# In-projection of 24 chunk pairs by seven block products in place of eight, and query norms spread over five heads

## The chip, the core and the metric

The kernel runs on one core of a Trainium2 chip. Its time is the device time of one launch in microseconds (us), lower is better. One execution was also taken by the hardware profiler; all rows below are from it. Engines: PE is TensorE (PEld its weight loads), DVE is VectorE, ACT is ScalarE, POOL is GpSimd; SP only issues transfers (DMAs).

## What is computed

One step of a one-layer hybrid encoder on 1024 prompt tokens and 32 sample tokens (1056 together), width 1024. Everything starts with one wide projection of the normalised, modulated input `h`:

```
h = _rms(x, p['norm_gain']) * (1 + scale[:, None, :]) + shift[:, None, :]
(qkv_raw, z_a, beta_raw, alpha_raw, q_raw, ckv_raw, kr_raw, z_b, g_a, g_b) = _split_in(h @ p['w_in'])
o_a, conv_new, s_new = _deltanet(qkv_raw, beta_raw, alpha_raw, conv_buf, s0, p)
o_b, ckv_new, kr_new = _mla(q_raw, ckv_raw, kr_raw, pos, past_ckv, past_kr, p)
u_a = o_a * jax.nn.silu(z_a)
u_b = o_b * jax.nn.silu(z_b)
merged = jax.nn.sigmoid(g_a) * (u_a @ p['w_o_dn']) + jax.nn.sigmoid(g_b) * (u_b @ p['w_o_mla'])
y = x + gate[:, None, :] * (merged @ p['w_out'])
```

`scale`, `shift` and `gate` come from `c @ w_ada`. `qkv_raw` (3072 columns) also goes through a causal convolution of four taps; the rest of the 9296 columns does not. All data are float32.

## The kernel before

The program runs in stages, and at the end of the first ones all five engines wait for each other (`meet`). **Pass 1** (`*_pass01`) computes the projection transposed, channels on partitions and tokens in columns, and stores it to a scratch in HBM. **Latents** builds keys and values of the attention branch. **Attention** runs 9 query blocks of 8 heads; block i has 128(i+1) keys. Then come the delta branch, the output projections and the result.

In pass 1 a float32 number is held as two parts of the type float32r, a rounded `hi` and the rest `lo`. The input is in `HH` and `HL`; 256 columns of `w_in` (a pair of chunks of 128 channels) come by DMA from POOL's queue into one half of `Wraw`, ACT rounds them into `WH`, DVE subtracts and writes `WL`. A product then takes three matmuls, WL·HH, WH·HL and WH·HH (`pe_chunk`). One chunk is 8 blocks of the inner dimension x 3 parts x 3 PSUM banks of 352 tokens = 72 matmuls, each with its own weight load. There are 73 chunks: 24 with convolution, 48 without, and a narrow one of 80 channels (`MISC`: beta, alpha, rotary key) at the end. Two sets of three PSUM banks alternate. For the 48 plain chunks ACT copies PSUM to `stage` with the activation (line 2249), and SP stores it. For the 24 others ACT copies to `Xr`, DVE convolves (lines 2461 and 2464), ACT applies silu. POOL copies the taps and edges.

The 1024 gate columns of `w_ada` are summed by DVE (`gate_products`, in two halves, early in pass 1) and finished on PE with 16 tiny products (line 2361) after the last plain chunk. The weights `w_uk` and `w_uv` of the latents are also loaded during pass 1; ACT and DVE split `w_uk` there, and `w_uv` at the beginning of latents (lines 341 and 346).

In attention, DVE computes the norms of the next block's queries in three parts (`dve_q_norms`) after heads 2, 3 and 4 of a block (1, 2, 3 of the first), between the row maxima that each head's softmax waits for. PE's first scores of a block wait until both halves of its rotated queries are copied (`s_qe`, line 697).

Of the kernel before, what the change touches and what calls it, by code (L numbers as in the profile page):

```python
# [14 lines left out]
F32 = mybir.dt.float32  # L15
# [6 lines left out]
P = 128  # L22
D = 1024
# [85 lines left out]
def build(nc, a, o, scr, ctx):  # L109
# [17 lines left out]
    p1 = ExitStack()  # L127
    Wraw = sb(p1, "Wraw", [P, 4, KD, 256])
    HH = sb(p1, "HH", [P, KD, TOK], F32R)
    HL = sb(p1, "HL", [P, KD, TOK], F32R)  # L130
    WH = sb(p1, "WH", [P, 2, KD, 256], F32R)
    WL = sb(p1, "WL", [P, 2, KD, 256], F32R)
    R = sb(p1, "R", [P, 9, D])
    rows = sb(p1, "rows", [P, 2, P])
    NHF = 4
    hf = sb(p1, "hf", [P, NHF, 512])
    modr = sb(p1, "modr", [2, 2, 512])
    G = sb(p1, "G", [P, KD, 2])
    xst = sb(p1, "xst", [P, 3, 9])
    Rf = R[:, :, :].rearrange("p a b -> p (a b)")  # L140
# [11 lines left out]
    assert edo + 144 + 2 * P <= 9 * D  # L152
# [15 lines left out]
    s_xn = sem("x_normalised")  # L168
# [28 lines left out]
    gacc = Rf[:, 0:2 * D].rearrange("p (s n) -> p s n", s=2)  # L197
# [111 lines left out]
    def sp_latents(sp):  # L309
        sp_lraw(sp, 0, 0)  # L310
        for t in range(2):
# [20 lines left out]
    def u_raw(i):  # L332

        return Wraw[:, 2 + i % 4 // 2, KR * (i % 2):KR * (i % 2) + KR]
# [13 lines left out]
    def sp_w_u(sp, i):  # L348
        w = a["w_uk"] if i < 4 else a["w_uv"]
        if i >= 4:  # L350
            sp.wait_ge(s_ul, i - 3)
# [133 lines left out]
    def act_latents(act):  # L485
        act.activation(colB[:, B_KN:B_KN + 1], colB[:, B_KN:B_KN + 1], ACT.Copy, scale=colB[:, B_QN:B_QN + 1])
        for i in range(4, 8):
            act_u_hi(act, i)
# [3 lines left out]
        act_lat_hi(act, 0, 0)  # L492
        act_lat_squares(act, 1)
# [54 lines left out]
    def dve_latents(dve):  # L548
# [17 lines left out]
        for i in range(4, 7):  # L566
            dve_u_lo(dve, i)
        dve_latent(dve, 0, 0)
        dve_lat_lo(dve, 0, 0)
        dve_u_lo(dve, 7)  # L570
# [288 lines left out]
    def dve_q_norms(dve, i, part):  # L859

        ss, rs, root = qst[:, 0], qst[:, 1], qst[:, 2]
        if part == 0:
            dve.wait_ge(s_r7, max(turn[("q", i, n)] for n in range(3)) + 1)
            dve.tensor_reduce(ss[:, 0], qsq[:, 0:H * HD].rearrange("p (h n) -> p h n", h=H), AX.X, ALU.add)
            dve.tensor_reduce(ss[:, 1], qsq[:, H * HD:H * QH].rearrange("p (h n) -> p h n", h=H), AX.X, ALU.add)
            dve.drain()
            dve.tensor_scalar(ss[:, 0], ss[:, 0], 1.0 / HD, EPS, ALU.mult, ALU.add)
            dve.tensor_scalar(ss[:, 1], ss[:, 1], 1.0 / ROPE, EPS, ALU.mult, ALU.add)
            dve.drain()
        elif part == 1:  # L870
            if i:
                dve.wait_ge(s_qrr, i)
            rsqrt(dve, rs.rearrange("p a b -> p (a b)"), root.rearrange("p a b -> p (a b)"), ss.rearrange("p a b -> p (a b)"))
# [79 lines left out]
    def dve_attention(dve):  # L953
# [3 lines left out]
        for x in range(NX + 3):  # L957
# [1073 lines left out]
    def sp_pass01(sp):  # L2031
# [8 lines left out]
        for c in range(2):  # L2040
            sp.wait_ge(s_adam, 7 + c)
            w_ada(2 + c, 2 * D + 256 * c)
# [3 lines left out]
        def stores(first, last):  # L2046
            with sp.Fori(first, last) as it:
                for c in range(2):
                    sp.wait_ge(s_stage, 2 * it + c + 2)
                    sp.dma_start(scr["proj"][bass.ds(2 * it + c, 1)].rearrange("a p n -> (a p) n"), stage[:, c]).then_inc(s_store[c], 16)  # L2050
        stores(0, 14)
        sp.wait_ge(s_mod, 5)
        for c in range(2):
            w_ada(2 + c, 2 * D + 512 + 256 * c)
        stores(14, 18)
        sp.wait_ge(s_mod, 6)
        for i in range(4):
            sp_w_u(sp, i)
        stores(18, 26)
        for i in range(4, 8):  # L2060
            sp_w_u(sp, i)
        stores(26, (NCHUNK - 1) // 2)
        sp_latents_early(sp)
        sp.wait_ge(s_stage, NCHUNK + 1)
        sp.dma_start(scr["proj"][C_MISC, 0:MISC], stage[0:MISC, 0]).then_inc(s_store[0], 16)
        sp.wait_ge(s_edc, 2)
# [19 lines left out]
    def pool_pass01(pool):  # L2086
# [23 lines left out]
        with pool.Fori(0, NCV // 4) as it:  # L2110
            for c in range(4):
# [413 lines left out]
```

## Time and profile before

| | us |
|---|---|
| median of 3 runs (lowest to highest) | 2055.53 (2055.16 to 2058.75) |
| the profiled execution: time, span of its instructions | 2056.78, 2055.1 |
| pass 1, up to the meeting of the engines | 927.4 |
| PE busy with matmuls, share of the span | 1950.7, 95% |
| DVE, ACT, POOL busy | 880.0, 682.9, 199.9 |

Matmuls are pipelined and their ends are modelled, so the busy time of PE says that it was fed, not how fast it went; the distance from one matmul to the next does.

### The profile page before, as it was taken

The page shows a single profiled execution, that of the slowest core. Times are in us where ns is not written, and L with a number is a line of the kernel's source. Part 1 is how long each engine was busy: PE and PEld are TensorE (multiplying, and loading weights), DVE is VectorE, ACT ScalarE, POOL GpSimd, SP SyncE. Part 2 cuts the span into 40 slices and gives each one's busy share as a digit, 9 for nine tenths or more (in the row PEclk, how much of TensorE's full clock was granted, in tenths as well). Part 3 has the DMA queues.
Part 4 walks back from the last instruction along what each step waited for, and adds up shares of the span by engine and source line. Part 5 has one row for each costly group of instructions (what it writes and reads, how often), then busy time and mean ns, then how long its engine had stood idle before and what let it go on. Part 6 is the DMA issues. An engine that isn't in the chain of part 4 may idle for free.

```text
span 2055.1 us, 32030 instructions
## 1 busy us (share of the span) xinstructions
PE 1950.7 (95%) x12263; PEld 1801.2 (88%) x12263; DVE 880.0 (43%) x1933; ACT 682.9 (33%) x1491; POOL 199.9 (10%) x258
## 2 busy tenths in 40 slices
PE   7899999999999999998998798997999999999998
PEld 3899999999999999996775677776999998899877
DVE  3654545221101001006653656554767767443333
ACT  3433333112112122213332454335577665220110
POOL 0121211001000000000002221111201010000000
PEclk9999999999999999999999999999999999999999
DMA  8222232424222322111102221105123225433321
GB/s 316 85 88 98 87 113 93 159 87 139 96 103 93 128 98 89 70 58 56 47 21 66 73 63 46 48 21 175 42 63 103 83 63 202 162 113 107 103 83 66
DMA packets 154032, 195.66 MB, mean 95 GB/s; under 512 B 9457, under 2 KB 125214, under 8 KB 153932
## 3 DMA queue, kind: packets, MB, share of 16 engines
q1 hardware_dynamic: 142444, 151.85, 22.1%
q0 software_dynamic: 10224, 38.13, 5.5%
q10 hardware_dynamic: 1264, 4.39, 0.5%
q8 instruction: 58, 0.95, 0.2%
q14 instruction: 42, 0.34, 0.1%
HBM read 134.15 MB, written 60.19 MB: 95 GB/s over the span
## 4 chain that ended last, share of the span: by engine, by line
PE 83%; issue 5%; DVE 4%; DMA 3%; ACT 2%; POOLq 1%; DVEq 1%; POOL 1%; PEld 0%; PEldq 0%; SPq 0%; ACTq 0%
PE PS L2280 42%; PE PS L1508 10%; PE PS L1329 9%; PE PS L386 5%; PE PS L1432 5%; PE PS L1513 3%; PE PS L729 2%; PE PS L704 2%; PE PS L2299 1%; PE PS L717 1%; DMA Wraw<-in_w_ada 1%; DMA fr<-scratch_u 1%; ACT E L1680 1%; PE PS L690 1%; PE PS L706 1%
## 5 line engine op out<-in xcount | busy, mean ns | idle before, releaser
L2280 PE MATMUL PS<-HH,WL 128*128 128x352 f32 (+1 forms) x1752 | 380.8, 326 | 5.3 <-DVE WL L2436 5.3
L2280 PE MATMUL PS<-HH,WH 128*128 128x352 f32 (+1 forms) x1752 | 378.8, 324 | 0.0
L2280 PE MATMUL PS<-HL,WH 128*128 128x352 f32 (+1 forms) x1752 | 378.6, 324 | 0.0
L2280 PEld LDWEIGHTS PS<-HH,WL 128*128 128x128 f32 (+1 forms) x1752 | 298.6, 189 | 5.9 <-DVE WL L2436 5.4
L2280 PEld LDWEIGHTS PS<-HH,WH 128*128 128x128 f32 (+1 forms) x1752 | 301.4, 188 | 0.5
L2280 PEld LDWEIGHTS PS<-HL,WH 128*128 128x128 f32 (+1 forms) x1752 | 298.0, 188 | 0.4
L2436 DVE TENSOR_TENSOR WL<-Wraw,WH 128x2048 fp32r<-128x2048 f32 x37 | 84.8, 2292 | 475.3 <-ACT WH L2204 475.2
L2249 ACT ACTIVATE R<-PS 128x1056 f32<-128x1056 f32 x48 | 50.5, 1053 | 405.6 <-PE PS L2280 405.6
L805 ACT ACTIVATE pr<-PS,amx,qsc 128x128 f32<-128x128 f32 (+8 forms) x72 | 57.9, 804 | 160.3 <-DVE amx L951 156.2
L1508 PE MATMUL PS<-WT,QL 128*128 128x128 f32 x832 | 102.1, 276 | 1.3 <-DVE QL L1911 0.9
L1508 PEld LDWEIGHTS PS<-WT,QL 128*128 128x128 f32 x832 | 97.0, 192 | 2.9 <-DVE QL L1911 2.9
L729 PE MATMUL PS<-V,pT 128*128 128x128 f32 (+1 forms) x624 | 86.1, 282 | 12.3 <-ACT pT L821 11.9
L2464 DVE SCALAR_TENSOR_TENSOR R<-R 128x1059 f32<-128x1059 f32 x72 | 95.2, 1322 | 5.4
L1736 ACT ACTIVATE WT<-PS 128x512 f32<-128x512 f32 x104 | 62.0, 597 | 97.0 <-PE PS L1508 97.0
L729 PEld LDWEIGHTS PS<-V,pT 128*128 128x128 f32 (+1 forms) x624 | 77.7, 193 | 18.1 <-ACT pT L821 16.2
L1329 PE MATMUL PS<-FH,VL 128*128 128x352 f32 x384 | 85.3, 331 | 7.4 <-DVE FL L1262 4.6
L704 PE MATMUL PS<-kT,qT 128*128 128x512 f32 (+4 forms) x208 | 85.7, 495 | 6.9 <-DVEq L932 6.9
L1329 PE MATMUL PS<-FL,VH 128*128 128x352 f32 x384 | 84.4, 329 | 0.0
L1329 PE MATMUL PS<-FH,VH 128*128 128x352 f32 x384 | 83.7, 326 | 0.0
L1911 DVE COPY_PREDICATED QL<-lev,PS 128x512 f32<-128x512 int32 x90 | 60.6, 726 | 34.1 <-PE PS L1513 34.0
L1329 PEld LDWEIGHTS PS<-FH,VL 128*128 128x128 f32 x384 | 66.2, 191 | 9.3 <-issue 3.8
L2204 ACT ACTIVATE WH<-Wraw 128x2048 fp32r<-128x2048 f32 x37 | 70.8, 1913 | 6.9 <-issue 6.8
(308 smaller groups left out, 3092.9 us busy)
## 6 DMA issues: line engine op xcount, KB each, us to landing
scratch_proj<-R SPq DMA_DIRECT2D x72, 576.0 KB, 2.8
Wraw<-in_w_in POOLq DMA_DIRECT2D x30, 1024.0 KB, 5.4
QKV<-scratch_proj SPq DMA_DIRECT2D x27, 512.0 KB, 5.5
Wraw<-in_w_ada SPq DMA_DIRECT2D x12, 1024.0 KB, 6.9
fr<-scratch_u SPq DMA_DIRECT2D x16, 528.0 KB, 5.7
gr<-scratch_proj SPq DMA_DIRECT2D x16, 528.0 KB, 3.8
qT<-scratch_proj SPq DMA_DIRECT2D x9, 512.0 KB, 5.2
zb<-scratch_proj SPq DMA_DIRECT2D x18, 256.0 KB, 3.1
```

Source lines behind the costliest of these rows:

```text
L386: last = pe.matmul(PS[:, bank + half], l[:, slot, r], u[:, r, 512 * half:512 * half + 512], start=(r == 0 and begin), stop=(r == KR - 1 an ...
L704: pe.matmul(out, qT[:, (i + 1) % 3, h], kT[:, h, c:c + w], start=True, stop=False)
L729: last = pe.matmul(PS[:, 6, (h % 4) * P:(h % 4 + 1) * P], pT[0:w, x % 2, k], V[0:w, base // P + k, h * HD:(h + 1) * HD], start=(k == 0), s ...
L1329: last = pe.matmul(PS[:, n % 2 + 2 * b, 0:TB], w[l % 2][:, k, (n % 2) * P:(n % 2) * P + P], u[:, k, b * TB:(b + 1) * TB], start=(k == 0 an ...
L1432: last = pe.matmul(PS[:, 4 * slot + h], m[:, slot, k], w[:, k, 512 * h:512 * h + 512], start=(k == 0 and fst), stop=(k == KD - 1 and m is ...
L1508: last = pe.matmul(hs(out, h), lhs(h), rhs(h), start=True, stop=True)
L1513: last = pe.transpose(hs(out, h), src(h), ident)
L1736: act.activation(WT[:, g], bank(g, 3), ACT.Copy).then_inc(d_x, 1)
L2204: act.activation(WH[:, s], Wraw[:, s], ACT.Copy).then_inc(s_whi, 1)
L2280: last = pe.matmul(PS[0:m, psum + b, 0:TB], w[:, s, k, c * P:c * P + m], h[:, k, b * TB:(b + 1) * TB], start=(k == 0 and first), stop=(k = ...
L2436: dve.tensor_tensor(WL[:, s], Wraw[:, s], WH[:, s].bitcast(F32), ALU.subtract).then_inc(s_wlo, 1)
L2464: last = dve.scalar_tensor_tensor(cv, x[:, i:i + XW - 3], wt[:, i:i + 1], cv, ALU.mult, ALU.add)
```

## The change

The 48 plain chunks are taken as 24 pairs. For a pair the weights (256 channels x 1024) and the input (1024 x 1056) are each cut into 2 x 2 blocks, and the four block results are made from seven products of block sums in place of eight products (Strassen's scheme in Winograd's form). Each of the seven is 128 channels x 512 x 528 tokens: 4 inner blocks x 3 parts x 2 banks of 264 columns = 24 matmuls (`pe_product`), 168 for a pair where there were 144 of 352 columns.

- **Left sums** (of weights, for each pair): POOL, 4 additions of 128x512; ACT and DVE split seven factors of 128x512 (`factor_hi`, `factor_lo`) where they split one 128x2048.
- **Right sums** (of the input, once): POOL `right_sums` and DVE `right_split` during convolution chunks 12 to 19; the last of the four sums, `right_last`, on DVE within the first pair, since its place in `HH` and `HL` comes free only then.
- **Results**: DVE copies or adds each product out of PSUM (8 additions and copies of 528 columns for a pair), ACT applies the activation in place in `stage`.
- **Moved**: the narrow chunk comes after chunk 21, ahead of chunks 22 and 23. The gate columns are loaded in eight pieces of 128 by SP during pairs 15 to 22 and summed by DVE at the end of pairs 16 to 23. `w_uk` is loaded in the last pair and split at the start of latents, and `w_uv` is loaded and split after that.
- **Attention**: query norms in five parts after heads 0 to 4, the next block's query transposes one head earlier, and the wait for rotated queries once per half block.

The core of the diff:

```diff
+    def pe_product(pe, f):
+        for kk in range(4):
+            for w, part, first in ((WLf, 0, True), (WHf, 1, False), (WHf, 0, False)):
+                for b in range(2):
+                    last = pe.matmul(PS[:, PRODUCT_BANK[f] + b, 0:TQ], left_block(w, f)[:, kk], right_block(f, part, kk)[:, b * TQ:(b + 1) * TQ],
+                                     start=(kk == 0 and first), stop=(kk == 3 and w is WHf and part == 0))
+        last.then_inc(s_chunk, 1)
...
+        with pe.Fori(0, NQ1) as q:
+            for f in range(7):
+                pe.wait_ge(s_wlo, 7 * q + WLO0 + f + 1)
+                pe.wait_ge(s_evac, 8 * q + EV0 + (-2, -1, 0, 0, 1, 2, 3)[f])
+                if f == 6:
+                    pe.wait_ge(s_hl, NG + 16)
+                pe_product(pe, f)
...
+    def left_factor(q, f):
+        w = raw_of(q)
+        return (w[:, 0:4, 0:P], left_raw[:, 1], w[:, 4:8, 0:P], left_raw[:, 0], left_raw[:, 2], left_raw[:, 3], w[:, 4:8, P:256])[f]
...
+        def right_last(kk):
+            t, b = cv[:, 0:TH2], cv[:, TH2:TOK]
+            dve.tensor_tensor(t, t_piece(1, 0, kk).bitcast(F32), t_piece(1, 1, kk).bitcast(F32), ALU.add)
+            dve.tensor_tensor(b, HH[:, kk + 4, 0:TH2].bitcast(F32), HL[:, kk + 4, 0:TH2].bitcast(F32), ALU.add)
+            dve.drain()
+            dve.tensor_tensor(t, t, b, ALU.subtract)
+            dve.drain()
+            dve.tensor_copy(t_piece(3, 0, kk), t)
+            dve.drain()
+            dve.tensor_tensor(t_piece(3, 1, kk), t, t_piece(3, 0, kk).bitcast(F32), ALU.subtract).then_inc(s_hl, 1)
+            dve.drain()
...
+        def factor_lo(q, f):
+            dve.wait_ge(s_whi, WHI0 + 7 * q + f + 1)
+            hi, lo = left_block(WHf, f).bitcast(F32), left_block(WLf, f)
+            if f == 6:
+                dve.scalar_tensor_tensor(lo, left_factor(q, f), -1.0, hi, ALU.mult, ALU.subtract).then_inc(s_wlo, 1)
+            else:
+                dve.tensor_tensor(lo, left_factor(q, f), hi, ALU.subtract).then_inc(s_wlo, 1)
...
+        for q in range(NQ1):
+            more = q + 1 < NQ1
+            factor_lo(q, 6)
+            dve.wait_ge(s_chunk, CH0 + 7 * q + 1)
+            dve.wait_ge(s_store[0], 16 * (q + 14))
+            dve.tensor_copy(by_half(stage[:, 0, 0:TH2]), in_product(0)).then_inc(s_evac, 1)
+            if more:
+                factor_lo(q + 1, 0)
+            dve.wait_ge(s_chunk, CH0 + 7 * q + 2)
+            dve.drain()
+            dve.tensor_tensor(by_half(prodU), by_half(stage[:, 0, 0:TH2]), in_product(1), ALU.add).then_inc(s_evac, 1)
+            dve.wait_ge(s_chunk, CH0 + 7 * q + 3)
+            dve.drain()
+            dve.tensor_tensor(by_half(stage[:, 0, 0:TH2]), by_half(stage[:, 0, 0:TH2]), in_product(2), ALU.add).then_inc(s_evac, 1)
+            if q == 0:
+                dve.wait_ge(s_stage, 1 + NC1)
+                for kk in range(2):
+                    right_last(kk)
+            if more:
+                for n in range(1, 3):
+                    factor_lo(q + 1, n)
+            dve.wait_ge(s_chunk, CH0 + 7 * q + 4)
+            dve.drain()
+            dve.tensor_tensor(by_half(prodV), by_half(prodU), in_product(3), ALU.add).then_inc(s_evac, 1)
+            if q == 0:
+                for kk in range(2, 4):
+                    right_last(kk)
+            if more:
+                factor_lo(q + 1, 3)
+            dve.wait_ge(s_chunk, CH0 + 7 * q + 5)
+            dve.wait_ge(s_store[1], 16 * (q + 13))
+            dve.drain()
+            dve.tensor_tensor(by_half(stage[:, 1, TH2:TOK]), by_half(prodV), in_product(4), ALU.add).then_inc(s_evac, 1)
+            dve.tensor_tensor(by_half(prodU), by_half(prodU), in_product(4), ALU.add).then_inc(s_evac, 1)
+            if more:
+                factor_lo(q + 1, 4)
+            dve.wait_ge(s_chunk, CH0 + 7 * q + 6)
+            dve.tensor_tensor(by_half(stage[:, 0, TH2:TOK]), by_half(prodV), in_product(5), ALU.add).then_inc(s_evac, 1)
+            if more:
+                factor_lo(q + 1, 5)
+            dve.wait_ge(s_chunk, CH0 + 7 * q + 7)
+            dve.drain()
+            dve.tensor_tensor(by_half(stage[:, 1, 0:TH2]), by_half(prodU), in_product(6), ALU.add).then_inc(s_evac, 1)
+            dve.drain()
+            if q >= 16:
+                gate_products(q - 16)
...
+        def gate_products(j):
+            dve.wait_ge(s_ada[2], 16 * (3 + j))
             for k in range(KD):
...
+        def left_sums(q):
+            w = raw_of(q)
+            a11, a12, a21, a22 = w[:, 0:4, 0:P], w[:, 4:8, 0:P], w[:, 0:4, P:256], w[:, 4:8, P:256]
+            pool.wait_ge(s_raw[(q + 1) % 2], 16 * ((q + 13) // 2 + 1))
+            pool.tensor_tensor(left_raw[:, 0], a21, a22, ALU.add)
+            pool.drain()
+            pool.tensor_tensor(left_raw[:, 1], left_raw[:, 0], a11, ALU.subtract)
+            pool.tensor_tensor(left_raw[:, 2], a11, a21, ALU.subtract)
+            pool.drain().then_inc(s_xn, 1)
+            pool.tensor_tensor(left_raw[:, 3], a12, left_raw[:, 1], ALU.subtract)
+            pool.drain().then_inc(s_xn, 1)
...
+        def load_pair(q):
+            pool.wait_ge(s_wlo, 14 + q if q < 2 else WLO0 + 7 * (q - 1))
...
+            if q >= 15 and q < 23:
+                j = q - 15
+                sp.wait_ge(s_mod, 4 + j)
+                if j == 0:
+                    sp.wait_ge(s_conv, NCV + 2)
+                    sp.wait_ge(s_edge, NCV + 2)
+                sp.dma_start(graw, a["w_ada"][0, :, 2 * D + P * j:2 * D + P * j + P].rearrange("(k p) n -> p k n", p=P)).then_inc(s_ada[2], 16)
+            if q == NQ1 - 1:
+                sp.wait_ge(s_wlo, WLO0 + 7 * NQ1)
+                for i in range(4):
+                    sp_w_u(sp, i)
+            for c in range(2):
+                n = 2 * l + c
+                sp.wait_ge(s_stage, n + 3)
+                sp.dma_start(scr["proj"][n], stage[:, c]).then_inc(s_store[c], 16)
...
+        def factor_hi(q, f):
+            if f == 0:
+                act.wait_ge(s_raw[(q + 1) % 2], 16 * ((q + 13) // 2 + 1))
+            if f in (1, 5):
+                act.wait_ge(s_xn, SUM0 + 2 * q + (1 if f == 1 else 2))
+            if q == 0:
+                act.wait_ge(s_chunk, CH0 - 2 if f < 4 else CH0)
+            else:
+                act.wait_ge(s_chunk, CH0 + 7 * (q - 1) + f + 1)
+            act.activation(left_block(WHf, f), left_factor(q, f), ACT.Copy, scale=-1.0 if f == 6 else 1.0).then_inc(s_whi, 1)
...
-        for step, phase, kind, part in ((-1, LATE, "q", 0), (0, LATE, "q", 1), (1, LATE, "q", 2), (6, EARLY, "b", 0), (6, LATE, "b", 1)):
+        for step, phase, kind, part in ((-2, LATE, "q", 0), (-1, LATE, "q", 1), (0, LATE, "q", 2), (6, EARLY, "b", 0), (6, LATE, "b", 1)):
...
-        if h == 0:
-            pe.wait_ge(s_qe, 2 * (i + 1))
+        if h % 4 == 0:
+            pe.wait_ge(s_qe, 2 * i + h // 4 + 1)
...
+    Q_NORMS = (("nope", "rope", "root", "refine", "scales"), ("rope", "nope", "root", "refine", "scales"))
-            first = 2 if x >= H else 1
-            if first <= x % H <= first + 2 and x // H + 1 < NQ:
-                dve_q_norms(dve, x // H + 1, x % H - first)
+            if x % H < 5 and x // H + 1 < NQ:
+                dve_q_norms(dve, x // H + 1, Q_NORMS[min(x // H, 1)][x % H])
```

In the rows of instructions that follow, `front` is the buffer that was `R`: it holds `stage`, `cv` and the sums. Names in brackets are the semaphores waited for.

PE, the plain chunks in the loop of before, the beginning of one chunk:

```order
L2356 ISA [waits w_lo_ready]
L2280 MATMUL PS<-HH,WL 128x352 [waits chunk_evacuated]
L2280 MATMUL PS<-HH,WL 128x352 x2
L2280 MATMUL PS<-HL,WH 128x352 x3
L2280 MATMUL PS<-HH,WH 128x352 x3
```

and the loop over the pairs now, the end of the first product and the beginning of the second:

```order
L2463 MATMUL PS<-HH,WL 128x264 x2
L2463 MATMUL PS<-HL,WH 128x264 x2
L2463 MATMUL PS<-HH,WH 128x264 x2
L2555 REGISTER_ALU
L2556 REGISTER_ALU [waits w_lo_ready]
L2463 MATMUL PS<-right_factors_a,WL 128x264 [waits chunk_evacuated]
L2463 MATMUL PS<-right_factors_a,WL 128x264
L2463 MATMUL PS<-right_factors_a,WH 128x264 x4
```

Runs of three matmuls of 352 columns became runs of two of 264, and the two waits come every 24 matmuls where they came every 72 or 144.

DVE in the first pair, from the third result of PSUM to the fourth (line 2690 is `factor_lo`, 2674 to 2681 are `right_last`):

```order
L2723 TENSOR_TENSOR front<-front,PS 128x528 [waits chunk_in_psum]
L2674 TENSOR_TENSOR front<-right_factors_a 128x528 [waits chunk_staged]
L2675 TENSOR_TENSOR front<-HH,HL 128x528
L2677 TENSOR_TENSOR front<-front 128x528
L2679 CAST HH<-front 128x528
L2681 TENSOR_TENSOR HL<-front,HH 128x528
L2674 TENSOR_TENSOR front<-right_factors_a 128x528
L2675 TENSOR_TENSOR front<-HH,HL 128x528
L2677 TENSOR_TENSOR front<-front 128x528
L2679 CAST HH<-front 128x528
L2681 TENSOR_TENSOR HL<-front,HH 128x528
L2690 TENSOR_TENSOR WL<-Wraw,WH 128x512 [waits w_hi_ready] x2
```

Ten operations now stand between two results in this pair, and ten more follow the fourth result; the seventh product waits for the last of them.

SP, the end of pass 1 now (line 2145 loads 128 gate columns, 2153 stores a chunk):

```order
L2145 DMA front<-in_w_ada 128x8x128 [waits edges_kept,chunk_convolved,modulation_steps_of_vector_engine]
L2153 DMA scratch_proj<-front 128x1152 [waits chunk_staged] x2
L2145 DMA front<-in_w_ada 128x8x128 [waits modulation_steps_of_vector_engine]
L2153 DMA scratch_proj<-front 128x1152 [waits chunk_staged] x2
L2145 DMA front<-in_w_ada 128x8x128 [waits modulation_steps_of_vector_engine]
```

The gate loads stood ahead of the stores and early in pass 1; now each stands ahead of the two stores of its pair, and from the second on waits for DVE's gate sums at the end of that same pair.

## Rows read from the trace of the kernel before

**Rows 1.** The page: busy time of PE; granted clock in 40 slices.

```profile
PE 1950.7 (95%) x12263; PEld 1801.2 (88%) x12263; DVE 880.0 (43%) x1933; ACT 682.9 (33%) x1491; POOL 199.9 (10%) x258
PEclk9999999999999999999999999999999999999999
```

**Rows 2.** Windows: us; busy us and instructions per engine; clock, DMA share, GB/s.

```profile
70.30:350.00 279.70, 279.70 (x1729) 279.70 (x1730) 142.06 (x114) 94.06 (x145) 56.90 (x113) 1.00 0.25 94
350.00:905.00 555.00, 555.00 (x3432) 555.00 (x3430) 82.91 (x62) 110.66 (x85) 29.20 (x33) 1.00 0.29 105
905.00:927.00 22.00, 18.46 (x107) 16.83 (x105) 0.17 (x1) 2.42 (x4) 0.00 (x0) 0.84 0.28 75
...
1112.00:1200.00 88.00, 65.86 (x395) 52.20 (x394) 50.81 (x165) 36.43 (x99) 24.40 (x25) 0.94 0.24 68
```

**Rows 3.** The chain that ended last, in order: start, us, what.

```profile
70.25 834.86 PE PS L2280 x5157
905.11 4.33 PE PS L2361 x32
909.43 13.82 PE PS L2280 x72
...
942.15 8.34 PE PS L386 x36
...
1423.89 3.57 PE PS L1508 x32
```

**Rows 4.** PE's timeline in attention: start, us, engine, line, operation.

```profile
1143.43 0.28 PE L706 MATMUL PS<-krH,qrT 128*128 128x256 f32 x1
1143.55 0.61 PE L729 MATMUL PS<-V,pT 128*128 128x128 f32 x4
```

**Rows 5.** Weight loads by form: busy us, mean ns, idle before.

```profile
L2280 PEld LDWEIGHTS PS<-HH,WH 128*128 128x128 f32 x1728 | 297.2, 188 | 0.0
```

**Rows 6.** ACT by form.

```profile
L2204 ACT ACTIVATE WH<-Wraw 128x2048 fp32r<-128x2048 f32 x37 | 70.8, 1913 | 6.9 <-issue 6.8
...
L821 ACT ACTIVATE pT<-PS 128x512 f32<-128x512 f32 x40 | 23.5, 588 | 1.4 <-PE PS L717 1.4
...
L2239 ACT ACTIVATE R<-PS 128x704 f32<-128x704 f32 x24 | 18.2, 760 | 64.6 <-PE PS L2280 58.5 <-POOLq L2119 6.1
```

**Rows 7.** DVE by form.

```profile
L2464 DVE SCALAR_TENSOR_TENSOR R<-R 128x1059 f32<-128x1059 f32 x72 | 95.2, 1322 | 5.4
...
L2429 DVE SCALAR_TENSOR_TENSOR R<-Wraw,colA,R 128x512 f32<-128x512 f32 x28 | 19.8, 748 | 1.0
...
L2416 DVE TENSOR_TENSOR HL<-hf,HH 128x512 fp32r<-128x512 f32 x16 | 11.1, 692 | 1.2
...
L2414 DVE CAST HH<-hf 128x512 fp32r<-128x512 f32 x16 | 6.8, 423 | 12.3 <-ACT hf L2198 12.2
...
L976 DVE COPY pT<-PS 128x512 f32<-128x512 f32 x8 | 5.5, 689 | 5.8 <-PE PS L717 5.8
```

**Rows 8.** POOL by form.

```profile
L839 POOL TENSOR_TENSOR qrr<-qrx 128x512 f32<-128x512 f32 x9 | 11.5, 1276 | 1.3
```

**Rows 9.** DMA issues: queue, count, KB each, median us to landing.

```profile
scratch_proj<-R SPq DMA_DIRECT2D x72, 576.0 KB, 2.8
Wraw<-in_w_in POOLq DMA_DIRECT2D x30, 1024.0 KB, 5.4
...
zb<-scratch_proj SPq DMA_DIRECT2D x18, 256.0 KB, 3.1
```

**Rows 10.** The start of latents, timeline of ACT and DVE.

```profile
927.63 3.88 ACT L341 ACTIVATE UVH<-Wraw 128x1024 fp32r<-128x1024 f32 x4
...
929.48 3.50 DVE L346 TENSOR_TENSOR UVL<-Wraw,UVH 128x1024 fp32r<-128x1024 f32 x3
```

**Rows 11.** Waits: who waited for whom, us in total, times, longest.

```profile
PEld PS L704 <- DVEq L932: 8.8, 8, 1.2
```

More of the change, by code:

```diff
@@ L492, in act_latents @@
         act_lat_hi(act, 0, 0)
+        for i in range(4, 8):
+            act_u_hi(act, i)
+        act.drain()
         act_lat_squares(act, 1)
@@ L569, in dve_latents @@
         dve_lat_lo(dve, 0, 0)
-        dve_u_lo(dve, 7)
+        for i in range(4, 8):
+            dve_u_lo(dve, i)
         dve.wait_ge(s_lb, 1)
@@ L2147, in pool_pass01 @@
-        pool.wait_ge(s_wlo, 2 * done + 1)
-        for c, lo, n, landed in ((0, COL_BA, BA, s_misc), (BA, COL_KR, ROPE, s_raw[0])):
-            pool.dma_start(Wraw[:, 0, :, c:c + n], a["w_in"][0, :, lo:lo + n].rearrange("(k p) n -> p k n", p=P)).then_inc(landed, 16)
-            pool.wait_ge(s_misc, 16 * 11)
+                edges(c % 2, bass.ds(n, 1), n + 3, n + 1)
+        for n in range(12, NCV):
+            late = int(n >= 22)
+            if n == 18:
+                misc_load()
+            elif n == 20:
+                load(12, 0, 256 * 11)
+            elif n == 22:
+                load_pair(0)
+                pool.wait_ge(s_hl, NG + 12)
+                left_sums(0)
+            elif n % 2 == 0:
+                load(n // 2 + 2, n // 2 % 2, 256 * (n // 2 + 2 - n // 2 % 2))
+            if 12 <= n < 20 and n % 2 == 0:
+                right_sums((n - 12) // 2)
+            edges(n % 2, slice(n, n + 1), n + 3 + late, n + 1)
@@ L2152, in _ @@
+        load_pair(1)
+        for q in range(1, NQ1):
+            pool.wait_ge(s_wlo, WLO0 + 7 * (q - 1) + 6)
+            left_sums(q)
+            if q + 1 < NQ1:
+                load_pair(q + 1)
     @block.gpsimd
@@ new lines, in act_pass01 @@
+        with act.Fori(0, 5) as it:
+            for c in range(4):
+                if c % 2 == 0:
+                    split_hi(1 - c // 2, 2 * it + c // 2 + 1, 16 * (it + c // 2 + 1))
+                conv_evac(c % 2, 3 * (c % 2), 4 * it + c, 0, 16 * (2 * it + c // 2 + 1))
+        split_hi(1, 11, 16 * 6)
+        for c in range(2):
+            conv_evac(c, 3 * c, 20 + c, 0, 16 * 11)
+        split_hi(0, 12, 16 * 7)
+        act.wait_ge(s_chunk, CH0 - 2)
+        act.wait_ge(s_store[0], 16 * 12)
@@ new lines, in convolve @@
+        def convolve(c, evac, staged):
+            x = Xr[:, c]
+            wt = wcv[:, c]
+            dve.wait_ge(s_evac, evac)
+            dve.wait_ge(s_stage, staged)
+            dve.tensor_scalar(cv, x[:, 0:XW - 3], wt[:, 0:1], None, ALU.mult)
+            dve.drain()
+            for i in range(1, CONV):
+                last = dve.scalar_tensor_tensor(cv, x[:, i:i + XW - 3], wt[:, i:i + 1], cv, ALU.mult, ALU.add)
+                if i < CONV - 1:
+                    dve.drain()
+            last.then_inc(s_conv, 1)
@@ new lines, in factor_lo @@
+        def factor_lo(q, f):
[5 more added lines that the diff above has]
+                dve.tensor_tensor(lo, left_factor(q, f), hi, ALU.subtract).then_inc(s_wlo, 1)
+        with dve.Fori(0, 3) as it:
+            for c in range(4):
+                if c % 2 == 0:
+                    split_lo(1 - c // 2, 2 * it + c // 2 + 1)
+                convolve(c % 2, 4 * it + c + 3, 4 * it + c + 1)
@@ new lines, in dve_pass01 @@
+        for n in range(12, NCV):
+            late = int(n >= 22)
+            if n % 2 == 0:
+                split_lo((n // 2 + 1) % 2, n // 2 + 1)
+            if n == 22:
+                for f in range(4):
+                    factor_lo(0, f)
+            if n < 20 and n % 2 == 1:
+                right_split((n - 12) // 2)
+            convolve(n % 2, n + 3 + late, n + 1 + late)
+        for f in range(4, 6):
+            factor_lo(0, f)
+        dve.wait_ge(s_edge, NCV + 2)
+        dve.drain()
```

361 lines of the change are left out of this document (212 added, 149 removed).

## The prediction, made before the changed kernel ran

> **What bounds the kernel now.** I read the page first: PE is busy 95% of the span at nearly full clock [rows 1], and a busy PE may still wait inside, so the next view is the chain in order of time [rows 3]. Its longest piece is the in-projection: 5157 matmuls in 834.86 us without a break, 161.9 ns from one 352-column matmul to the next. The windows say the same for the plain chunks: between 350 and 905 us PE has no idle time, while DVE is busy 82.9, ACT 110.7 and POOL 29.2 of 555 us [rows 2]. So in pass 1 the number and length of matmuls set the end, and the others have room for more work. A chunk of 72 costs 11.66 us.
>
> **What a matmul of 264 columns costs.** The trace has none. 512 columns of the same type go every 231.7 ns (36 in 8.34), 352 every 161.9 [rows 3]; the line through both gives 123.5 at 264. A single 256-column matmul of the type in attention is followed after 0.12 us by the next one [rows 4], against 120.0 on that line. A floor: 128-column matmuls with a load each go every 111.6 (32 in 3.57), and 1-column ones too, bound by their load, every 135 in the mean (32 in 4.33, partly at a lower clock) [rows 3]. I take 122.5, between 120.5 and 126. A pair is then 168 x 0.1225 = 20.6 us where it was 23.3.
>
> A rule speaks against this. The Trainium skill (TensorE: Matmul & The Clock Gate, The mechanism) says that a weight load overlaps a running matmul only if it goes to another row group, and (LDWEIGHTS) that 128 columns load in 107 ns. All loads here fill all rows, so by that load and stream would add up: an estimate of 217 ns at 264 columns, 24 pairs in 875 us against 560 before, a kernel near 2370 us. The trace disagrees: load and stream of 352 columns would be 254 ns, and 161.9 is measured.
>
> **The sum, term by term** (minus is faster).
>
> *Products:* 48 x 11.66 = 559.7 us become 24 x 20.58 = 493.9: **-65.8**; bounds -74 and -52 by the two ends above.
>
> *Left sums, factors, results, per pair.* POOL: four additions of 1.28 [rows 8] and a load, 6 us. ACT: seven roundings of 0.59 and up to four activations of about 0.6 [rows 6], 6.5 us. DVE: seven subtractions of 0.69 and eight reads of PSUM of 0.70 [rows 7], 10.5 us with the drains. All lie beside 20.6 us of PE, and a product's banks are needed again only three products (8.8 us) later, two of the next pair's: **0**. Without that cover it would be DVE's 10.5 us a pair.
>
> *Right sums beside chunks 12 to 19.* POOL six additions of 1.32, 8 us for two chunks; DVE three casts of 0.43 and three subtractions of 0.71, 3.5 us. DVE has been busy 142 and POOL 57 of 280 us there [rows 2]. ACT's read of an even chunk waits 2 us longer for POOL's edges, and PE needs those banks only 11.66 us later: **0**; without that cover four times some 6 us.
>
> *Transition.* The split for chunks 22 and 23 waits for chunk 21's silu on ACT and has one chunk's time, not two: 0.6. PE's first product waits until ACT has emptied chunk 23, 0.76 + 0.43 and a little [rows 6]: 1.6. **+2.2**.
>
> *First pair.* From the end of chunk 23, DVE's way to the last right sum: ACT's read 1.5, convolution 5.0 (three of 1.32 and a multiply, [rows 7]), silu 1.3, rounding 0.6; then DVE's three subtractions 2.1, product 0 0.7, a subtraction 0.7, products 1 and 2 1.4, two subtractions 1.4, product 3 0.8, and four `right_last` of 3.4 (four operations of 0.70, a cast 0.43, drains), 13.6: 29.1 us. PE is through six products after 1.6 + 6 x 2.94 = 19.2. It waits 9.8. The end of pass 1 shows what a stretch with little PE work costs besides: with the granted clock at 0.84 in that window [rows 2] the narrow chunk of 72 took 13.82 [rows 3], not 11.66. I add 2.2: **+12**, bounds 9 and 15.
>
> *Gate sums.* An operation of 128 columns is by the line through 512 (0.748) and 1059 (1.322) [rows 7] 0.35 us; two for each of 8 blocks and drains, 5.0 us at the end of pairs 16 to 23. SP loads the next columns only after it, and the pair's stores stand behind that load on its queue; DVE's first write into `stage` of the next pair waits for the store. So there is a ring: load and store land, then DVE: eight results 5.7, six subtractions 4.2, waits for ACT 0.5 and 1.2, gate sums 5.0 = 16.6, then SP again. The store alone lands in 2.8; the load is two of 256 KB with 3.1 each in pieces of the same size [rows 9]. Overlapped in one queue 4.5, one after the other up to 8, with POOL's 1 MB beside them for some. I take 5: a ring of 21.6 against 20.6 us of PE, 1 us in each of 7 pairs: **+7**, bounds 0 and +28.
>
> *End of pass 1.* Before: gate products 4.33, narrow chunk 13.82 [rows 3], and the rest up to the meeting at 927.4: 22.3 us after the last plain chunk. Now the narrow chunk is inside at 11.7, but after the last product come DVE's last result 0.9, gate sums 5.0, gate products 4.3 to 6.8, and 3 for transposes, copies and two issues: 14.5. 11.7 + 14.5 - 22.3 = **+3.9**, bounds 2 and 7.
>
> *Latents.* ACT splits four pieces before the first latent as before (3.88), DVE four, not three (3.50): +1 [rows 10]. The `w_uv` pieces come right after, four of 1.0 and 1.2 on ACT and DVE, in front of the second latent; DVE's first keys come some 2.4 us later in all. Later steps have idle time on DVE: **+2.4**, bounds 0 and 6.
>
> *Attention.* The wait of PE for the second half of rotated queries is 8.8 us in 8 places [rows 11]. It goes; in late blocks PE is the bound and gets it back, in the early ones the softmax ring takes some: -5. The norms: DVE spends 6 to 7 us on them for each next block. In 1112 to 1200 PE is busy 65.9 of 88 us [rows 2], and idle because scores wait for a DVE in three heads of eight; in five smaller parts more lies in DVE's slack: -4. **-9**, bounds 0 and -17.
>
> Sum: -65.8 + 2.2 + 12 + 7 + 3.9 + 2.4 - 9 = -47.3. Against the profiled execution's 2056.8 us that is 2009.5; the median of the runs is 1.2 lower, so I forecast **2008**.
>
> **Rivals.**
> - *Weight loads set the pace (slower).* A load is recorded with 188 ns [rows 5]; if one could not begin before the last was done, 4032 x 0.188 = 758 us, +264 against my term, 2272. Already 161.9 is less than 188, and 111.6 occurs. It turns the sign where a matmul takes over 122.5 + 47.3 / 4.032 = 134.2 ns. The skill's rule above is this rival at its worst. Chance 0.04; a pace between 126 and 134 (2022 to 2055), 0.07.
> - *The gate load holds the stores.* If load and store land one after the other, beside POOL's load, the ring is 24.6 or more, +4 us in 7 pairs: 2029, and to 2040 if the load is slower still. For it: all three transfers begin in the same 2 us. Against: the pieces are spread over 16 engines and the queue is short. 0.13.
> - *Attention gains nothing.* The moved parts delay other maxima, and PE's wait goes to the next exponential: 2017. For it: in the early blocks PE idles in nearly each head. 0.15.
> - *My sum:* 0.61, by itself from 1998 to 2020.
>
> **How the numbers follow.** 2008 is the likeliest case. Below, the pace at 120.5 and attention at its bound give 1994. Above, I go to 2030, which takes in attention without gain, the gate ring at 24.6 and a pace of 126; what lies outside is some 0.15. What this kernel's measurement can tell from no change is about 0.2%, 4 us. Slower by more: the weight loads 0.03 and unseen stalls 0.01; no change 0.02; faster 0.94.
>
> **What would show each step.** Right: in the new loop 24 matmuls every 2.9 us, with no idle time of PE in pairs 1 to 15; one wait of PE for DVE of about 10 us in the first pair; waits of about 1 us before the fifth product of pairs 17 to 23, whose releaser is DVE behind a store; PE's wait for DVE at the first scores of each block gone; pass 1 ending near 885. Wrong: a step from matmul to matmul over 130 ns; idle time of PE in most pairs; waits of 4 us or more in the last pairs; attention as long as before.

## The result and the profile after

The changed kernel takes 2043.87 us (median of 4 runs, 2043.08 to 2044.63) beside 2055.81 for the one before: ratio 0.9934, 95% interval 0.9922 to 0.9947. It is faster by 0.7%, with an interval that leaves out 1, but by 12 us where 47 were forecast, and it lies outside the range, above its end of 2030.

The page of the changed kernel, busy time of PE and the granted clock in 40 slices (for [rows 1]):

```profile
PE 1903.3 (93%) x12839; PEld 1752.5 (86%) x12839; DVE 1160.8 (57%) x2409; ACT 719.8 (35%) x1642; POOL 377.8 (18%) x378
...
PEclk9999999899999998888999899998999999999999
```

PE is busy for 47 us less, but the clock, which before stood at 9 in every slice (90% or more of full speed), is at 8 in the slice of the first pair (from 357 us), in four from 766 to 970, and in two of attention and its end (from 1124 and 1379). The chain in order of time says what lies in the first of these (for [rows 3]; start, us, what):

```profile
333.64 23.55 PE PS L2453 x144
358.72 9.05 PE PS L2463 x72
388.59 330.20 PE PS L2463 x2688
731.71 5.53 DMA scratch_proj<-front
738.08 8.29 PE PS L2463 x48
759.28 5.45 DMA scratch_proj<-front
765.58 8.21 PE PS L2463 x48
...
914.31 7.00 PE PS L2564 x32
...
1083.01 4.51 DMA qT<-scratch_proj
...
1413.76 3.57 PE PS L1594 x32
```

The loop over the pairs begins at 358.7. PE waits up to 388.6 for its seventh product, then the loop runs without a break to pair 16, and from there a store of `scratch_proj` stands in the chain every 27 us. Cut to the pairs between, clear of the stretch behind the first wait, the chain gives the pace, 121.7 ns from one matmul to the next, or 20.45 us a pair:

```profile
401.97 312.05 PE PS L2463 x2564
```

Who PE waited for between 330 and 925 us (us in total, times, longest):

```profile
PE PS L2463 <- DVE front L2715: 28.5, 7, 4.7
PE PS L2463 <- DVE HL L2681: 12.1, 1, 12.1
PE PS L2564 <- DVE gate_sums_c L2627: 6.6, 1, 6.6
PE PS L2463 <- ACT front L2370: 1.5, 1, 1.5
```

Line 2715 is DVE's copy of product 0 into `stage`, line 2681 the last operation of `right_last`. The windows (for [rows 2]; us, busy us and instructions of PE, PEld, DVE, ACT, POOL; clock, DMA share, GB/s) set the pairs without and with gate sums side by side, and one stretch right behind a wait:

```profile
390.00:715.00 325.00, 325.00 (x2655) 325.00 (x2654) 174.56 (x240) 91.37 (x144) 116.19 (x90) 0.99 0.32 113
715.00:907.00 192.00, 163.52 (x1228) 162.07 (x1227) 122.69 (x216) 46.52 (x75) 35.55 (x29) 0.89 0.28 101
```

```profile
738.00:746.00 8.00, 7.92 (x47) 7.92 (x48) 6.56 (x11) 2.96 (x5) 0.00 (x0) 0.69 0.28 111
```

In the first 325 us PE has no idle time, as forecast. In the 192 us after them it idles for 28.5 and runs at a mean clock of 0.89. Behind the first of the seven waits, which is 4.7 us long, 48 matmuls take 8.29 us in the chain, 173 ns each. The six waits of pairs 17 to 22 are 4.3 to 4.7 us long, and a stretch of this kind follows each; the last is 1.2 us long, and behind it 72 matmuls take 9.03 us, 125 ns each.

What fills the 27 us is seen between the copies of product 0 of pairs 19 and 20, at 792.25 and 819.60. DVE first takes the eight results and subtracts six factors; from the last result on its rows are all shown (start, us, engine, line, operation, idle before and its releaser):

```profile
792.25 0.71 DVE L2715 COPY front<-PS 128x528 f32<-128x528 f32 x1 [5.40 <-DMA scratch_proj<-front]
...
804.18 0.70 DVE L2752 TENSOR_TENSOR front<-front,PS 128x528 f32<-128x528 f32 x1
804.97 0.77 DVE L2625 TENSOR_SCALAR front<-front,colA 128x128 f32<-128x128 f32 x2
805.81 7.80 DVE L2627 SCALAR_TENSOR_TENSOR front<-front,colA 128x128 f32<-128x128 f32 x14
813.53 0.68 DVE L2688 SCALAR_TENSOR_TENSOR WL<-Wraw,WH 128x512 fp32r<-128x512 f32 x1
819.60 0.71 DVE L2715 COPY front<-PS 128x528 f32<-128x528 f32 x1 [5.38 <-DMA scratch_proj<-front]
```

POOL at the time of the gate sums, and SP's issues after them:

```profile
804.18 1.28 POOL L2231 TENSOR_TENSOR Wraw<-Wraw 128x512 f32<-128x512 f32 x1 [16.13 <-DVE WL L2690]
805.69 1.30 POOL L2233 TENSOR_TENSOR Wraw<-Wraw 128x512 f32<-128x512 f32 x1 [0.23 <-issue]
806.95 1.35 POOL L2234 TENSOR_TENSOR Wraw<-Wraw 128x512 f32<-128x512 f32 x1
808.47 1.29 POOL L2236 TENSOR_TENSOR Wraw<-Wraw 128x512 f32<-128x512 f32 x1 [0.18 <-issue]
```

```profile
813.64 0.39 SPq L2145 DMA_DIRECT2D front<-in_w_ada  x1
814.46 0.81 SPq L2153 DMA_DIRECT2D scratch_proj<-front  x2
```

The durations of the gate operations of the first four turns, least, median and longest in ns:

```profile
L2627 DVE SCALAR_TENSOR_TENSOR front<-front,colA x56: 340/351/1392, 723.5 to 813.3; 128x128 f32<-128x128 f32 x56
```

A gate operation takes 0.35 us, just as worked out, but three in each of these pairs take 1.3 to 1.4, as long as the addition that POOL has in hand. So the sums end at 813.6, 8.6 us after they began. Only then does SP issue the next gate load, and the pair's stores behind it; the first store lands 5.05 us after its own issue (5.53 and 5.45 in other turns of the chain) and 5.9 us after SP began with the load. Then DVE copies product 0, and PE may begin its fifth product.

The last turn has the gate sums without the additions, since POOL has no pair left to prepare. All its 14 operations of this kind take 0.34 to 0.35 us, the sums last 5.3 us (886.74 to 892.05), and the turn 24.0 us, from the copy at 873.90 to that at 897.93. Half of them, by form (busy us, mean ns, idle before):

```profile
L2627 DVE SCALAR_TENSOR_TENSOR gate_sums_b<-front,colA,gate_sums_b 128x128 f32<-128x128 f32 x7 | 2.5, 352 | 0.5
```

### The profile page after: what moved, and what is told of

It reads as the page before. It is cut to its first block, busy times and chain, and to the rows that moved or that the text cites. A ratio compares the mean times of both kernels' runs of the same rounds, so it can differ in the third digit from the quotient of the medians.

```text
span 2042.9 us, 34109 instructions
## 1 busy us (share of the span) xinstructions
PE 1903.3 (93%) x12839; PEld 1752.5 (86%) x12839; DVE 1160.8 (57%) x2409; ACT 719.8 (35%) x1642; POOL 377.8 (18%) x378
## 4 chain that ended last, share of the span: by engine, by line
PE 75%; DVE 8%; issue 5%; DMA 4%; ACT 3%; DVEq 2%; POOLq 1%; POOL 0%; PEld 0%; SPq 0%; PEldq 0%; ACTq 0%
PE PS L2463 20%; PE PS L2453 14%; PE PS L1594 10%; PE PS L1415 9%; PE PS L1518 5%; PE PS L458 4%; PE PS L1599 3%; PE PS L807 3%; PE PS L782 2%; DMA scratch_proj<-front 2%; PE PS L795 1%; PE PS L2481 1%; DMA Wraw<-in_w_ada 1%; DVEq L2629 1%; ACT E L1766 1%
## 5 line engine op out<-in xcount | busy, mean ns | idle before, releaser
L2463 PE MATMUL PS<-right_factors_a,WH 128*128 128x264 f32 x1008 | 174.1, 290 | 0.0
L2463 PE MATMUL PS<-HH,WL 128*128 128x264 f32 x768 | 157.9, 287 | 13.6 <-DVE HL L2681 12.1
L2463 PE MATMUL PS<-HH,WH 128*128 128x264 f32 x768 | 156.8, 286 | 0.0
L2463 PE MATMUL PS<-HL,WH 128*128 128x264 f32 x768 | 156.7, 286 | 0.0
L2463 PE MATMUL PS<-right_factors_a,WL 128*128 128x264 f32 x576 | 124.3, 299 | 28.5 <-DVE front L2715 28.5
L2453 PE MATMUL PS<-HH,WL 128*128 128x352 f32 (+1 forms) x600 | 130.6, 326 | 5.7 <-DVE WL L2634 5.7
L2453 PE MATMUL PS<-HH,WH 128*128 128x352 f32 (+1 forms) x600 | 129.7, 324 | 0.0
L2453 PE MATMUL PS<-HL,WH 128*128 128x352 f32 (+1 forms) x600 | 129.6, 324 | 0.0
L2453 PEld LDWEIGHTS PS<-HH,WL 128*128 128x128 f32 (+1 forms) x600 | 101.7, 188 | 6.4 <-DVE WL L2634 6.1
L2453 PEld LDWEIGHTS PS<-HH,WH 128*128 128x128 f32 (+1 forms) x600 | 102.8, 187 | 0.3
L2453 PEld LDWEIGHTS PS<-HL,WH 128*128 128x128 f32 (+1 forms) x600 | 101.8, 187 | 0.2
```

The costliest lines, as they stand in the source:

```text
L2453: last = pe.matmul(PS[0:m, psum + b, 0:TB], w[:, s, k, c * P:c * P + m], h[:, k, b * TB:(b + 1) * TB], start=(k == 0 and first), stop=(k = ...
L2463: last = pe.matmul(PS[:, PRODUCT_BANK[f] + b, 0:TQ], left_block(w, f)[:, kk], right_block(f, part, kk)[:, b * TQ:(b + 1) * TQ], start=(kk ...
```

## The experiments

The kernel before, run again beside each group, has medians of 2056.8 to 2057.1 us, where it had 2055.8 beside the changed kernel, so a difference between the times of two groups carries about 1 us besides its interval.

**The stores ahead of the load.** In SP's loop over the pairs:

```diff
-            if q >= 15 and q < 23:
-                j = q - 15
-                sp.wait_ge(s_mod, 4 + j)
...
-                sp.dma_start(graw, ...).then_inc(s_ada[2], 16)
...
                 sp.wait_ge(s_stage, n + 3)
                 sp.dma_start(scr["proj"][n], stage[:, c]).then_inc(s_store[c], 16)
+            if q >= 15 and q < 23:
+                j = q - 15
+                sp.wait_ge(s_mod, 4 + j)
...
+                sp.dma_start(graw, ...).then_inc(s_ada[2], 16)
```

> The changed kernel (2043.9 us) with the two stores of a pair issued ahead of the gate load, not behind it. Theory A (in pairs 17 to 23 the stores wait for the gate sums of their own pair because the load that waits for them stands ahead on SP's queue): the ring opens, the seven waits of TensorE of 4.8 us and the low clock behind them go, pass 1 is some 38 us shorter: 2006 us. Rival B (VectorE simply has too much to do in these pairs with 8.7 us of gate sums): the pairs stay at 24 us or more in place of 20.6 and TensorE waits for the fifth product's bank without any store in the chain: 2025 us or more.

Measured 2002.03 us, 41.8 below the changed kernel (ratio to before 0.9735, interval 0.9711 to 0.9759). Its waits of PE:

```profile
PE PS L2463 <- DVE HL L2681: 12.0, 1, 12.0
PE PS L2564 <- DVE gate_sums_c L2627: 6.6, 1, 6.6
PE PS L2463 <- ACT front L2370: 1.6, 1, 1.6
PE PS L2463 <- DVE front L2715: 1.4, 4, 0.5
```

The waits for the copy of product 0 fall from 28.5 to 1.4 us, and no other wait of PE here moves by more than 0.1. Theory A holds; that DVE has too much to do (B) leaves 1.4 us of waits.

**One block of the gate sums.** `for k in range(KD)` in `gate_products` becomes `for k in range(1)`.

> The changed kernel with the gate sums over the first of eight blocks only (the gate is therefore another number); the load stays ahead of the stores. Theory A: a ring of 27.2 us loses 7.8 us of gate sums, is 19.4 and below the 20.6 us of TensorE: no wait, and 4.5 us less at the end of pass 1: 2002 us. Rival C (load and store on one queue, not the sums, hold VectorE up): the sums are off the path, pairs stay above 24 us: 2030 us or more.

Measured 1994.45 us (ratio 0.9692, interval 0.9669 to 0.9715). PE's waits for DVE in pass 1 behind the first pair:

```profile
PE PS L2564 <- DVE gate_sums_c L2625: 1.4, 1, 1.4
```

None for line 2715 is left, although the load still stands ahead of the stores, so C falls. Of the 7.6 us by which it is faster than the stores-first kernel, 5.2 are this wait at the end of pass 1, which was 6.6, and 1.4 the four waits left there; the last 1.0 is less than the spread of the runs.

**The wait without the load.**

```diff
-                sp.dma_start(graw, ...).then_inc(s_ada[2], 16)
+                if j == 0:
+                    sp.dma_start(graw, ...).then_inc(s_ada[2], 16)
+                else:
+                    sp.sem_inc(s_ada[2], 16)
```

> The changed kernel with SP's wait for the gate sums kept ahead of the stores, but with the load itself left out from the second piece on (the sums then read the first piece again). Theory A: the store lands in 2.8 us as elsewhere and not in 5.5, and SP saves 0.4 us of issue: the ring falls from 27.2 to some 24, 21 us less in all: 2022 us. Rival C (the load is what holds the stores): the waits go altogether: 2006 us. Rival D (only the wait counts, the load costs the store nothing): 2041 us.

Measured 2021.88 us (ratio 0.9828, interval 0.9806 to 0.9851): A's number. A store in its chain, and its waits (lines of that kernel are 3 higher):

```profile
753.88 2.78 DMA scratch_proj<-front
```

```profile
PE PS L2466 <- DVE front L2718: 13.9, 6, 3.4
```

Without the load ahead of it a store lands in 2.8 us, not 5.1 to 5.5. Taking the load out gives back half of the loss, 22.0 us, by the earlier landing of the store and SP's saved issue; the other 19.9 go when the stores no longer stand behind the wait either. These shares of one ring overlap with those of the other runs here and are not to be added up.

**POOL reads nothing beside the gate sums.** In `left_sums`, for the pairs from 17 on:

```diff
+            if q >= 17:
+                for n in range(4):
+                    pool.memset(left_raw[:, n], 0.0)
...
+                return
```

> The changed kernel with GpSimd's four left sums of pairs 17 to 23 replaced by fills with zero of the same four tiles (these pairs' results are therefore others); GpSimd then reads nothing from SBUF while VectorE forms the gate sums. Theory A2 (five of sixteen gate operations take 1.3 to 1.4 us and not 0.35 because GpSimd's additions run beside them): the gate sums fall from 8.7 to 5.2 us, the ring from 27.2 to 23.7, TensorE's seven waits become about 1.5 us: 24 us less, 2020 us. Rival: the long operations have another cause (the landing transfer, strided rows): 2044 us.

Measured 2021.27 us (ratio 0.9822, interval 0.9799 to 0.9844). The first 56 gate operations between 715 and 907 us, by form (busy us, mean ns, idle before), in the changed kernel:

```profile
L2627 DVE SCALAR_TENSOR_TENSOR front<-front,colA 128x128 f32<-128x128 f32 x56 | 29.4, 565 | 2.1
```

and in this one (lines 7 higher), with PE's waits:

```profile
L2634 DVE SCALAR_TENSOR_TENSOR front<-front,colA 128x128 f32<-128x128 f32 x56 | 17.2, 349 | 2.1
```

```profile
PE PS L2470 <- DVE front L2722: 13.9, 7, 2.7
```

The expectation counted five long operations in sixteen; the trace has three. POOL's fills are shorter than its additions, so most of the gate operations lie behind them, but the two of each pair that lie beside a fill take 0.35 us too. 565 ns become 349, and 22.6 us of the time go. A2 holds. This is what the Trainium skill (SBUF — State Buffer, Who interferes with whom) states: a VectorE instruction with two inputs in SBUF and a GpSimd instruction that reads SBUF need the same read port, and the later one stands until the other is done. The trace agrees: 1.31 to 1.40 us beside additions of 1.28 to 1.35.

**No last right sum.** Both pieces of code that call `right_last`, and the wait on `s_hl` ahead of product 6, are left out.

> The changed kernel (2043.9 us) with the four right_last left out and the seventh product of the first pair no longer waiting (every pair's seventh product is therefore another number). Theory: TensorE's wait of 12.2 us in the first pair goes, and with it 3.0 us of the 69 matmuls behind it, which went every 166 ns and not every 123: 2028.7 us. Rival: VectorE is late in the first pair anyway, since the last convolution ends when the third product does, and half the wait comes back in front of the fifth product: 2036 us.

Measured 2028.79 us (ratio 0.9859, interval 0.9839 to 0.9878). Of the two large waits one is left:

```profile
PE PS L2463 <- DVE front L2713: 28.6, 7, 4.9
```

The first pair's wait is worth 15.1 us, 12.1 as idle time and 3.0 as low clock, and no other takes its place.

**The attention part alone, and the half-block wait alone,** both on the kernel before. The second edit is only this:

```diff
-        if h == 0:
-            pe.wait_ge(s_qe, 2 * (i + 1))
+        if h % 4 == 0:
+            pe.wait_ge(s_qe, 2 * i + h // 4 + 1)
```

> The kernel before (2055.5 us) with the attention part of the change alone: norms in five parts, query transposes one head earlier, one wait for each half block. Theory: the stage took 338.5 us before and 330.8 in the changed kernel, and all of it comes from these edits: 2048 us. Rival: the difference of the stage came from the latents and the loads ahead of it: 2054 us or more.

> The kernel before with only the wait for rotated queries taken once per half block. The prediction's split of the attention term: 5 us for the wait, 4 for the norms, so 2050.5 us. Rival E: in the blocks where the softmax holds TensorE the time is waited for elsewhere, and the gain comes from the norms: 2054 us or more. Rival F: the wait is all of it: 2048 us.

Measured 2045.43 us for the whole part (ratio 0.9940, interval 0.9924 to 0.9956) and 2044.32 for the wait alone (0.9934, interval 0.9916 to 0.9952). The stage is read from the load of the first queries to the first big piece of the delta branch; the kernel before, then the whole part, then the wait alone:

```profile
1085.43 4.34 DMA qT<-scratch_proj
...
1423.89 3.57 PE PS L1508 x32
```

```profile
1085.24 4.40 DMA qT<-scratch_proj
...
1416.45 4.49 PE PS L1518 x32
```

```profile
1085.82 4.39 DMA qT<-scratch_proj
...
1413.06 5.20 PE PS L1508 x32
```

331.2 and 327.2 us, where it was 338.5. The wait per half block is all of the gain (F), and more than the 8.8 us of [rows 11]. The five parts and the earlier transposes gain nothing here; whether they cost the 4 us between the two profiles the times, 1.1 us apart with intervals of several, do not settle.

**The last right sum begun earlier,** on the stores-first kernel. `right_last` is split into `right_raw` (the sum, in place, in a free buffer) and `right_put` (hi and lo):

```diff
+            if n == 23:
+                dve.wait_ge(s_edge, NCV + 1)
+                dve.drain()
+                for kk in range(2):
+                    right_raw(kk, raw4[kk])
             convolve(n % 2, n + 3 + late, n + 1 + late)
+        dve.drain()
+        for kk in range(2):
+            right_put(kk, raw4[kk])
...
             if q == 0:
-                dve.wait_ge(s_stage, 1 + NC1)
-                for kk in range(2):
-                    right_last(kk)
+                for kk in range(2, 4):
+                    right_raw(kk, raw4[kk])
+                    right_put(kk, raw4[kk])
             if more:
-                for n in range(1, 3):
+                for n in range(int(q > 0), 3):
                     factor_lo(q + 1, n)
...
-            if q == 0:
-                for kk in range(2, 4):
-                    right_last(kk)
```

In the first pair the next pair's factor 0 is subtracted behind these sums too, no longer ahead of product 1.

> The kernel with the stores first (2002.0 us), and in it the last right sum begun earlier: for two of the four blocks VectorE forms the sum in the 5.4 us in which it waits for the last convolution chunk, and stores hi and lo while it waits for the first factors; the other two come right after the third result, ahead of the next pair's factors. Theory (the first pair's wait is VectorE's queue alone): the last piece is ready some 9 us earlier, at about 379 us and not 388.6, and the wait of 12.2 us falls to 3 and the low clock behind it by half: 1992 us. Rival: the three-operand sums meet GpSimd's left sums, or the next pair's late factors stop TensorE in the second pair: 1998 us or more.

Measured 1994.12 us (ratio 0.9695, interval 0.9677 to 0.9714), 7.9 below the stores-first kernel; its runs lie between 1990.75 and 1998.61, which leaves the last us open. The wait and the last piece's end:

```profile
PE PS L2463 <- DVE HL L2682: 3.4, 1, 3.4
```

```profile
379.18 0.71 DVE L2682 TENSOR_TENSOR HL<-front,HH 128x528 fp32r<-128x528 f32 x1
```

**The gate pieces one pair earlier,** on that kernel: loads in pairs 14 to 21, sums in 15 to 22, and PE's gate products wait only for their own bank.

```diff
-            if q >= 15 and q < 23:
+            if q >= 14 and q < 22:
...
-            if q >= 16:
-                gate_products(q - 16)
+            if 15 <= q < 23:
+                gate_products(q - 15)
...
-        pe.wait_ge(s_evac, EV0 + 8 * NQ1)
+        pe.wait_ge(s_evac, EV0 + 8 * NQ1 - 4)
```

> The kernel with the stores first and the last right sum begun earlier (1994.1 us), and in it the gate pieces one pair earlier (loads in pairs 14 to 21, sums at the end of pairs 15 to 22); the gate products of TensorE then wait only for their own bank. Theory (the end of pass 1 is a chain of VectorE's last gate sums, 5.7 us, and gate products at low clock, 7.0): the wait of 6.7 us goes and the products take some 5, pass 1 ends 8 us after its last matmul and not 16: 1986 us. Rival: the last store or the loads of the latents' weights hold the meeting of the engines: 1990 us or more.

Measured 1984.03 us (ratio 0.9652, interval 0.9639 to 0.9665), 10.1 below that kernel and the fastest here. The end of pass 1 in its chain:

```profile
828.34 29.47 PE PS L2463 x240
857.81 3.48 PE PS L2564 x32
```

The gate products follow at once, 3.5 us at a granted clock of 1.00, where they took 7.0 at 0.50.

**The old norms in it,** with the wait per half block kept.

> The kernel with the gate pieces earlier, and in attention the norms and query transposes of the kernel before; only the wait per half block is kept. Theory (the wait per half block is all of the attention's gain, the five parts and the earlier transposes give back some 3 us of attention): 1 to 3 us less than with the five parts. Rival: the runs of the two parts on the kernel before differ by chance, and the norms gain what was forecast (4 us): 4 us more.

Measured 1986.95 us (1982.13 to 1989.38) beside 1983.73 to 1986.80 for the kernel above: the spreads overlap, and neither side is shown. In the two profiled executions the attention stage is 328.2 us with the old norms (1024.76 to 1352.99) and 330.7 with the five parts (1023.06 to 1353.72), the same way round as 327.2 and 331.2 above; these are single executions.

## Why the prediction was too low

Against the profiles (2055.1 and 2042.9 us of span) the terms came out so:

| term | forecast | measured | from |
|---|---|---|---|
| products | -65.8 | -69.0 | 4032 x 121.7 ns against 559.7 |
| left sums, factors, results | 0 | 0 | no idle time from 390 to 715 us |
| transition | +2.2 | +1.9 | waits of 1.5 and, ahead of chunk 22, 0.4 |
| first pair | +12 | +15.1 | the run without the last right sum |
| gate ring | +7 | +42 | the run with the stores first |
| end of pass 1 | +3.9 | +5.3 | 907.7 to 923.6, and the narrow chunk's 11.7, less 22.3 |
| latents | +2.4 | +1.4 | 159.4 us to the first query load, before 158.0 |
| attention | -9 | -7.7 | 330.8 against 338.5 |
| after it | 0 | -2.1 | 629.1 against 631.2 |

The measured terms add up to -13; the spans differ by 12.2. What made the part after attention shorter no run here shows. The end of pass 1 is read from the first operation behind the meeting of the engines, here on ACT:

```profile
923.64 0.30 ACT L558 ACTIVATE colB<-colB 128x1 f32<-128x1 f32 x1 [1.06 <-SPq L377]
```

The step that failed is "Gate sums", a size and not a mechanism: the ring was forecast as it stands in the trace, load, store, DVE, and with it the place of the waits, ahead of the fifth product of pairs 17 to 23. Its length was put at 21.6 us, one above the 20.6 of PE; in the turn shown it is 27.3, and PE's pair 20.45. The waits of 4 us or more in the last pairs are a sign of being wrong that the prediction itself names. Four things were too small.

- The gate sums are 8.6 us and not 5.0. Of the 3.6, 3.0 are the three long operations. The rest is the sum as it was worked out: sixteen operations of 0.35 us are 5.6, and they take 5.6 in the run with the fills. The price of an operation came from rows of DVE [rows 7] beside which POOL had at most copies of a few columns in hand, while the change sets POOL's four additions beside the gate sums.
- Load and first store land in 5.9 us with SP's issue and not in 5: the load costs a store 2.3 to 2.7.
- DVE's results and factors with their waits take 12.7 us and not 11.6: it waits 0.6 and 1.5 us for ACT, close to the forecast, and 0.7 for PE's sixth product, which comes late behind PE's own wait.
- The low clock behind a wait, which the forecast added to the first pair alone, comes back behind six of the seven waits: of the 42 us only 28.5 are idle time.

The rows of the kernel before held a warning. There it is POOL that waits: each of its 24 copies of 4 columns in the convolution ends 0.04 or 0.05 us after the DVE operation that was running when it began. Here one takes 0.97 us, beside DVE operations that keep their 1.32, and the copy of 3 columns behind it takes 0.18:

```profile
233.18 0.97 POOL L2117 COPY R<-colA 128x4 f32 x1
234.10 0.18 POOL L2118 COPY R<-colB 128x3 f32 x1
```

The rival "the gate load holds the stores" was given 0.13 and at most 2040. It is part of what happened, since the run without the load gives back 22.0 us, but it made the load alone slower and left the gate sums at 5.0.

The first pair was right in its mechanism. DVE's way to the last sum took 31.3 us from the end of chunk 23 (357.2 to 388.5) and not 29.1; three of its operations met POOL's left sums there as well and took 1.2, 1.7 and 1.8 us.

That load and stream of a matmul would add up, or the load set the pace, is refuted: 121.7 ns at 264 columns, between the ends of 120.5 and 126. The low end of the range, 1994, is 1992 by the prediction's own terms; nothing hangs on it. Attention came out near its sum by a wrong split: 5 us were given to the wait per half block and 4 to the norms; the first is 10 or more by the run of it alone, and of the second no run shows a gain; that the sum came out near is luck.

## What to carry to other kernels

A ring that is forecast one us above its cover multiplies every error by the number of its turns: price such a ring from both sides, and ask first whether it can be opened; here moving two stores ahead of a waiting load was worth 42 us, more than three times what the whole change brought. Whatever a change gives to GpSimd must be laid beside what VectorE does at that moment, and VectorE's durations taken from a stretch where GpSimd has work of that kind. A wait that PE sees can cost more than its idle time: here 2.3 to 2.5 us more, at a lower clock, behind each of six waits of 4.3 to 4.7 us.

## What the runs showed of the hardware

- A 128x128 scalar_tensor_tensor of VectorE with two inputs in SBUF takes 0.35 us alone and 1.31 to 1.40 beside a GpSimd addition of 1.28 to 1.35; beside GpSimd's fills the two that fall there in each pair take 0.35.
- A GpSimd copy of 4 columns that begins while a VectorE operation of 1.32 us with two inputs in SBUF runs ends 0.04 or 0.05 us after it; the VectorE operation is not longer for it.
- Behind a wait of 4.7 us the granted clock was 0.69 over 8 us, and 48 matmuls took 173 ns each; behind the wait of 12.1 us 69 took 166 ns, and behind one of 1.2 us 72 took 125. At a clock of 1.00 they take 121.7.
- A store of 576 KB lands in 2.8 us alone and in 5.1 to 5.5 behind a load of 512 KB on the same queue.
